# A hybrid encoder layer pair on one core: two more value blocks fed unsplit to TensorE, and the order of splits, gelu parts, scans and small stores moved

## The chip, the core and the metric

The kernel runs on one core of a Trainium2 chip. TensorE (PE) multiplies, VectorE (DVE) and ScalarE (ACT) do the elementwise work, GpSimd (POOL) sums squares for the norms, and SyncE (SP) issues nearly all transfers. Each engine runs its own instructions in the order in which they are written and waits at counting semaphores. The metric is the time of one execution on the device, in microseconds (us); lower is better.

## The reference, cut to what matters

Input x is 256 tokens by 2048 channels, float32. There are two layers. Each is a normed mixer and a normed MLP of hidden size 8192, with residual sums. The change touches the first mixer only:

```python
proj = xn @ w_in                                   # 2048 -> q, k, v, u of 1024 each
q, k, v, u = jnp.split(proj, [A_WIDTH, 2 * A_WIDTH, 3 * A_WIDTH], axis=-1)
o_a = dilated_attention(heads(q), heads(k), heads(v), t5_table)      # 8 heads, T5 bias
y = (s5_direction(ug, ..., False) + s5_direction(ug, ..., True) + d_skip * ug)
y = jax.nn.gelu(y)                                 # S5 state space, both directions
o_b = y * jax.nn.sigmoid(y @ w_glu)
return jnp.concatenate([o_a, o_b], axis=-1) @ w_out
```

## The kernel before, in words

All weights stream through one ring of four slots, `raw[:, s]`, 512 KB each. A **block** is 256 columns of a weight matrix and has four **parts**, s = 0 to 3, each with four slices of 128 of the contraction. Part number n is 4 * block + s. SP loads part n into slot n % 4 once the part before it in that slot is done with (`raw_slot`).

Most parts are **split** before use: ACT copies `raw` to a rounded high half in `whl` (`high`, L556), DVE subtracts to get the low half (`low`, L926), and PE makes three reduced products in `sub_mm` (L1567). Parts of **native** blocks, J_NAT0 to J_NAT1 - 1, skip this: PE multiplies `raw` itself by the whole input `xf` (L1544), and no engine splits. `xf` is made once by `whole_input` on DVE, four additions, and lies over slots 0 and 1 of `whl`. So a split into these slots after the native blocks must wait until the last native part is used.

The first mixer goes through these stages:

- Blocks 0 to 3 project u, 4 to 7 q, 8 to 11 k, 12 to 15 v, 16 and 17 are the GLU (gate) matrix. Blocks 18 on are the output projection and all that follows.
- Meanwhile DVE makes the S5 weights and then the scan: 63 steps of four small operations (`scan`), a few after each part from (6, 3) to (12, 3) (`SCAN_SLOTS`). Between blocks 8 and 9 PE makes the local kernels (L1679), ACT takes them (`take_kernel`) and DVE adds the diagonal (`kernel_diagonal`, 0 and 1, counted in `k_mid`).
- SP writes these kernel rows to DRAM (`store_k`, tile `kst` to `k_rows`, waits for `k_mid` 6) and reads them back in another layout (`load_m`, to `mloc`, waits until the store has landed). Both stand in SP's one queue between weight loads, at a fixed n.
- In block 13, after each part, PE makes one **round** of chunk outputs (`chunk_outputs`, L1723 to L1732). Round 0 waits for the whole scan, `mloc` and the diagonal. ACT and DVE add the two directions (`take_round`, `round_sum`), SP stores the result (`store_y`) and loads it as `u` (`load_y`).
- Then the **head loop**, steps g = 0 to 7, one head of attention each. PE does parts of blocks 14 to 17 (`HEAD_SUBS`: two v parts a step, later two GLU parts), then scores of head g + 1, transposes of head g, and output of head g - 1. ACT and DVE split q, k and v of a head (`head_high`, `head_low`), do the softmax, split the weight parts, and do the gelu of the eight `u` tiles (`gelu_inner`, `gelu_tanhs`, `gelu_end`, and its split into `act` by ACT L839 and `gelu_low`). ACT also issues the T5 bias loads (`load_bias_a`). GLU part 64 needs gelu tiles 0 to 3 split and part 65 needs 4 to 7.

The whole order is written out by hand; no scheduler moves anything.

Of the kernel before, what the change touches and what calls it, by code (L numbers as in the profile page):

```python
# [18 lines left out]
HA = 8  # L19
# [7 lines left out]
NT = 8  # L27
# [30 lines left out]
J_NAT0, J_NAT1 = 8, 14  # L58
# [41 lines left out]


# [10 lines left out]
def build(nc, ins, out):  # L112
# [7 lines left out]
    with ctx:  # L120
# [180 lines left out]
        def _(sp):  # L301
# [110 lines left out]
            for n in range(4 * J_GLU + 8):  # L412
# [111 lines left out]
        def _(a):  # L524
# [229 lines left out]
            for s in range(4):  # L754
                high(0, J_HEADS, 0, s)
# [29 lines left out]
            def head_high(h):  # L785

                if h >= 3:
                    a.wait_ge(pv_mm, h - 2)
# [8 lines left out]
            high(0, J_HEADS + 1, 0, 0)  # L797
# [17 lines left out]

            for g in range(9):
                subs = HEAD_SUBS[g]
                for k, n in enumerate(subs):
                    if k == 1:
                        continue  # L820
                    high(0, n // 4 + 1, 0, n % 4)
                    if n in (4 * J_HEADS + 3, 4 * J_HEADS + 7):
                        take_tiles(n // 4)
# [6 lines left out]
                if len(subs) > 1 and subs[1] + 4 < 4 * J_OUT0 + 3:  # L830
                    high(0, subs[1] // 4 + 1, 0, subs[1] % 4)
                if g + 1 < HA:
                    scale_probs(g + 1)
                if g < 3:
                    gelu_tanhs(2 * g + 2)
                if g == 3:
                    for t in range(NT):
                        a.wait_ge(gelu_out, t + 1)
                        nc.scalar.activation(act[:, NT + t, 0, :], u[:, t], ACT.Copy, scale=0.5).then_inc(y_hi, 1)  # L839
# [3 lines left out]
                if g + 2 < HA:  # L843
                    head_high(g + 2)
# [76 lines left out]
        def _(v):  # L921
# [306 lines left out]
            def after(j, s):  # L1228
# [36 lines left out]
            for r in range(3):  # L1265
                round_sum(r)
            for s in range(4):
                low(0, J_HEADS, 0, s)
            round_sum(3)
# [69 lines left out]
            low(0, J_HEADS + 1, 0, 0)  # L1339
# [4 lines left out]
            for g in range(9):  # L1344
                subs = HEAD_SUBS[g]
                m = 2 * (g - 4)
                if subs:
                    low(0, subs[0] // 4 + 1, 0, subs[0] % 4)
# [8 lines left out]
                if len(subs) > 1 and subs[1] + 4 < 4 * J_OUT0 + 3:  # L1357
# [617 lines left out]
```

## Time and profile before

| | before |
|---|---|
| median of 3 runs | 2295.6 us (2291.8 to 2296.89) |
| the profiled execution's own time | 2293.73 us |
| its span in the trace | 2291.9 us |
| PE busy | 2225.5 us (97%) |
| DVE busy | 1561.0 us (68%) |
| ACT busy | 1025.6 us (45%) |
| first product of block 18 | at 369.2 us |

The page gives each engine's busy time as a share of the span. From block 18 on PE is busy all the time until the last few microseconds; what the change can alter lies ahead of it, in the first 370 us. "PEclk" in a row is the clock that TensorE was granted, as a share of 2.4 GHz; it has two levels, 1.00 and 0.50, and a value between is a mix over the stretch.

### The profile page before, as it was taken

The numbers are of one execution on the slowest core, as the hardware profiler recorded it, in microseconds if no ns is written. First come the engines' busy times: TensorE is split into PE (matmuls) and PEld (weight loads), VectorE is DVE, ScalarE is ACT, GpSimd is POOL, SyncE is SP. The second block draws the span as 40 slices with busy tenths as digits, with TensorE's granted clock in tenths as the row PEclk, the third lists the DMA queues.
The fourth block names the chain that finished last, engine by engine and source line by source line (L and its number), as shares of the span: only waits on it lengthen the run. The fifth ranks groups of instructions, "written<-read, shape, count | busy, mean of one in ns | idle before, by whom it ended". The sixth has DMA issues, their size and how long they took to land.

```text
span 2291.9 us, 40651 instructions
## 1 busy us (share of the span) xinstructions
PE 2225.5 (97%) x14099; PEld 1965.7 (86%) x14099; DVE 1561.0 (68%) x2549; ACT 1025.6 (45%) x1473; POOL 166.7 (7%) x154
## 2 busy tenths in 40 slices
PE   6989879999999999999999999999999999999997
PEld 6988668888888888888888888888888888888886
DVE  7799267676567567567677777767756756756765
ACT  6620157544444444444455444454444444444442
POOL 1000001400000000000320000141000000000022
PEclk9999889999999999999999999999999999999999
DMA  8535654657557557656665656565666565666563
GB/s 225 167 105 152 126 177 146 189 188 211 187 189 205 189 188 203 196 188 199 195 199 164 202 169 196 166 192 184 192 192 192 184 192 184 192 192 192 184 191 112
DMA packets 438953, 418.02 MB, mean 182 GB/s; under 512 B 49627, under 2 KB 434859, under 8 KB 438348
## 3 DMA queue, kind: packets, MB, share of 16 engines
q1 hardware_dynamic: 435952, 414.30, 59.3%
q10 hardware_dynamic: 2908, 2.51, 0.4%
q8 instruction: 55, 0.90, 0.2%
q14 instruction: 38, 0.31, 0.0%
HBM read 406.35 MB, written 10.39 MB: 182 GB/s over the span
## 4 chain that ended last, share of the span: by engine, by line
PE 92%; DVE 4%; ACT 1%; DMA 1%; issue 1%; SPq 0%; ACTq 0%; DVEq 0%
PE psum L1570 54%; PE psum L1571 27%; PE psum L1544 4%; PE psum L1567 2%; PE psum L1746 1%; DVE whl L926 1%; DVE fa L926 1%; ACT whl L556 0%; PE psum L1728 0%; DMA xin<-in_x 0%; SPq L382 0%; PE psum L1766 0%; DMA raw<-in_ab_w_in 0%; DVE ysum L926 0%; PE psum L1723 0%
## 5 line engine op out<-in xcount | busy, mean ns | idle before, releaser
L926 DVE TENSOR_TENSOR whl<-raw,whl 128x1024 fp32r<-128x1024 f32 x720 | 887.8, 1244 | 495.5 <-ACT whl L556 493.6
L556 ACT ACTIVATE whl<-raw 128x1024 fp32r<-128x1024 f32 x720 | 763.5, 1061 | 759.0 <-PE psum L1571 683.4
L1570 PE MATMUL psum<-act,whl 128*128 128x512 f32 x2560 | 892.4, 394 | 0.0
L1571 PE MATMUL psum<-act,whl 128*128 128x256 f32 x2560 | 713.6, 279 | 0.0
L1570 PE MATMUL psum<-hid,whl 128*128 128x512 f32 x2048 | 710.3, 392 | 0.0
L1570 PEld LDWEIGHTS psum<-act,whl 128*128 128x128 f32 x2560 | 479.7, 187 | 109.4
L1571 PE MATMUL psum<-hid,whl 128*128 128x256 f32 x2048 | 570.4, 279 | 0.0
L1571 PEld LDWEIGHTS psum<-act,whl 128*128 128x128 f32 x2560 | 482.1, 188 | 0.1
L1570 PEld LDWEIGHTS psum<-hid,whl 128*128 128x128 f32 x2048 | 383.5, 187 | 86.8
L1571 PEld LDWEIGHTS psum<-hid,whl 128*128 128x128 f32 x2048 | 385.5, 188 | 0.0
L567 ACT ACTIVATE half<-psum 128x256 f32<-128x256 f32 x344 | 113.7, 382 | 286.0 <-PE psum L1571 285.1
L926 DVE TENSOR_TENSOR ysum<-psum,half 128x256 f32<-128x256 f32 x344 | 130.0, 419 | 159.1 <-ACT half L567 159.0
L1567 PE MATMUL psum<-act,whl 128*128 128x256 f32 x768 | 98.3, 287 | 0.0
L489 POOL TENSOR_TENSOR ssum<-x 128x256 f32<-128x256 f32 x4 | 2.9, 728 | 1295.1 <-DVE x L926 1295.1
L1567 PEld LDWEIGHTS psum<-act,whl 128*128 128x128 f32 x768 | 94.4, 193 | 0.8 <-ACT unat L716 0.8
L1570 PE MATMUL psum<-whl,act 128*128 128x512 f32 x256 | 91.1, 398 | 0.0
L1570 PE MATMUL psum<-o_c,whl 128*128 128x512 f32 x256 | 89.2, 392 | 0.3 <-DVE o_c L926 0.3
L492 POOL TENSOR_TENSOR sq<-x 128x256 f32<-128x256 f32 x60 | 61.7, 1029 | 184.3 <-DVE x L926 179.7
L494 POOL TENSOR_TENSOR ssum<-ssum,sq 128x256 f32<-128x256 f32 x60 | 71.7, 1195 | 4.7
L1571 PE MATMUL psum<-whl,act 128*128 128x256 f32 x256 | 71.9, 281 | 0.0
L1571 PE MATMUL psum<-o_c,whl 128*128 128x256 f32 x256 | 71.6, 280 | 0.0
L1544 PE MATMUL psum<-xf,raw 128*128 128x256 f32 x256 | 59.8, 392 | 7.6 <-DVE xf L926 7.6
(203 smaller groups left out, 1798.0 us busy)
## 6 DMA issues: line engine op xcount, KB each, us to landing
raw<-in_mlp_w SPq DMA_DIRECT2D x512, 512.0 KB, 4.0
raw<-in_c_w_qkv SPq DMA_DIRECT2D x96, 512.0 KB, 4.5
raw<-in_ab_w_in SPq DMA_DIRECT2D x64, 512.0 KB, 4.0
raw<-in_ab_w_out SPq DMA_DIRECT2D x32, 512.0 KB, 4.2
raw<-in_c_w_out SPq DMA_DIRECT2D x32, 512.0 KB, 4.4
raw<-in_s_w_glu SPq DMA_DIRECT2D x8, 512.0 KB, 3.4
bias_c<-rpb_pad SPq DMA_DIRECT2D x64, 64.0 KB, 2.5
rpb_pad<-rpbw SPq DMA_DIRECT2D x4, 889.0 KB, 10.7
```

Source lines behind the costliest of these rows:

```text
L489: nc.gpsimd.tensor_tensor(ssum[:], x[:, 0], x[:, 0], ALU.mult).then_inc(ssum_done, 1)
L492: nc.gpsimd.tensor_tensor(sq[:], x[:, kt], x[:, kt], ALU.mult).then_inc(sq_done, 1)
L494: nc.gpsimd.tensor_tensor(ssum[:], ssum[:], sq[:], ALU.add).then_inc(ssum_done, 1)
L556: nc.scalar.activation(whl[:, s, :, 0, :], raw[:, s], ACT.Copy).then_inc(hi_done, 1)
L567: nc.scalar.activation(half[:, n], psum[:, banks + n, T:2 * T], ACT.Copy).then_inc(half_done, 1)
L926: return nc.vector.tensor_tensor(dst, s0, s1, op)
L1544: last = pe.matmul(psum[:, banks + n, 0:T], w, m, start=(kt == 0), stop=(kt == KT - 1), skip_group_check=True)
L1567: last = pe.matmul(bank[:, 0:T], w, m, start=(first and c == 0), stop=(final and c == 2), skip_group_check=True)
L1570: pe.matmul(bank, *big, start=first, stop=False, skip_group_check=True)
L1571: last = pe.matmul(bank[:, 0:T], *little, start=False, stop=final, skip_group_check=True)
L1746: last = pe.matmul(dst, w(wp), m(mp), start=(c == 0 and p == 0), stop=(c == len(products) - 1 and p == 2), skip_group_check=True)
```

## The change

Blocks 14 and 15 become native (J_NAT1 is 16), so their eight parts are no longer split. On DVE `whole_input` goes from the third part of block 7 to the first, and the two diagonals go six and five parts forward. On SP `store_k` goes from part 52 to 45, `load_m` from 54 to 47, and the last `store_y` and `load_y` come a little sooner. In the head loop the split of head 2 comes ahead of the loop. The GLU parts that used slots of split v parts are now split in step 3, four at once. The gelu tiles are split two a step from step 1, with the last two in step 4.

```diff
-J_NAT0, J_NAT1 = 8, 14
+J_NAT0, J_NAT1 = 8, 16
+HEAD_SPLITS = [()] * 3 + [(4 * J_GLU, 4 * J_GLU + 1, 4 * J_GLU + 2, 4 * J_GLU + 3)]
+HEAD_SPLITS += [(4 * J_GLU + 2 * g + 4, 4 * J_GLU + 2 * g + 5) for g in range(3)] + [(4 * J_GLU + 10,), ()]
...
-                if n == 52:
+                if n == 45:
                     store_k()
-                if n == 54:
+                if n == 47:
                     load_m()
                 for r in range(NROUND):
-                    if n == (56, 57, 58, 60)[r]:
+                    if n == (56, 57, 58, 59)[r]:
                         store_y(r)
-                    if n == (58, 59, 61, 62)[r]:
+                    if n == (58, 59, 59, 59)[r]:
                         load_y(r)
...
-            high(0, J_HEADS + 1, 0, 0)
+            head_high(2)
...
             for g in range(9):
...
+                splits = HEAD_SPLITS[g]
+                early = len(splits) // 2 if len(splits) > 1 else len(splits)
+                if 2 <= g < HA - 1:
+                    head_high(g + 1)
+                if g in (1, 3):
+                    take_tiles(J_HEADS + g // 2)
+                for n in splits[:early]:
+                    high(0, n // 4, 0, n % 4)
...
+                if 1 <= g <= 3:
+                    y_high(2 * g - 2)
...
-                if (j, s) == (10, 2):
+                if (j, s) == (9, 0):
                     kernel_diagonal(0)
-                if (j, s) == (11, 2):
+                if (j, s) == (10, 1):
                     kernel_diagonal(1)
...
-                    if j + 1 == J_NAT0 and s == 2:
+                    if j + 1 == J_NAT0 and s == 0:
                         whole_input()
...
+                if 2 <= g < HA - 1:
+                    head_low(g + 1)
+                for n in splits[:early]:
+                    low(0, n // 4, 0, n % 4)
+                if g == 4:
+                    gelu_low(6)
+                    gelu_low(7)
                 if g + 1 < HA:
                     scores(g + 1, (g + 1) % 2, ss_a, bias_a, False)
```

SP's queue around the kernel rows, before. "raw<-in_ab_w_in" is a weight part, x4 four of them; "t_rel" is the T5 table, stored after parts 41 and 45.

```order
40 L405 DMA t_rel<-t5sb 128x512
41 L334 DMA raw<-in_ab_w_in 128x4x256 x4
42 L405 DMA t_rel<-t5sb 128x512
43 L334 DMA raw<-in_ab_w_in 128x4x256 x3
44 L364 DMA k_rows<-kst 16x16x112 x4
45 L334 DMA raw<-in_ab_w_in 128x4x256 x2
46 L373 DMA mloc<-k_rows 16x32x64 x8
47 L334 DMA raw<-in_ab_w_in 128x4x256 x2
```

The same place in the changed kernel; its first row is the T5 store after part 45.

```order
40 L409 DMA t_rel<-t5sb 128x512
41 L368 DMA k_rows<-kst 16x16x112 x4
42 L338 DMA raw<-in_ab_w_in 128x4x256 x2
43 L377 DMA mloc<-k_rows 16x32x64 x8
44 L338 DMA raw<-in_ab_w_in 128x4x256 x2
45 L409 DMA t_rel<-t5sb 128x512
46 L338 DMA raw<-in_ab_w_in 128x4x256 x7
```

The four stores now stand ahead of the loads of parts 46 and 47, and the eight reads ahead of those of parts 48 and 49. Before, the parts behind them were 52 and 53, and 54 and 55.

DVE from the end of head step 3 to the scores of head 5, before: `act<-u` is the low half of a gelu tile (L929), `whl` the low half of a weight part.

```order
416 L926 TENSOR_TENSOR o_s<-psum,o_s 128x256
417 L929 SCALAR_TENSOR_TENSOR u<-inner,u 128x256 x2
418 L929 SCALAR_TENSOR_TENSOR act<-u,act 128x256 x8
419 L926 TENSOR_TENSOR qk_s<-qk_a,qk_s 128x2x256
420 L926 TENSOR_TENSOR v_s<-v_a,v_s 128x256
421 L926 TENSOR_TENSOR whl<-raw,whl 128x4x256
422 L929 SCALAR_TENSOR_TENSOR ss_a<-psum,bias_a 128x512
```

The same stretch in the changed kernel.

```order
409 L934 TENSOR_TENSOR o_s<-psum,o_s 128x256
410 L934 TENSOR_TENSOR whl<-raw,whl 128x4x256 x2
411 L937 SCALAR_TENSOR_TENSOR u<-inner,u 128x256 x2
412 L937 SCALAR_TENSOR_TENSOR act<-u,act 128x256 x2
413 L934 TENSOR_TENSOR qk_s<-qk_a,qk_s 128x2x256
414 L934 TENSOR_TENSOR v_s<-v_a,v_s 128x256
415 L934 TENSOR_TENSOR whl<-raw,whl 128x4x256
416 L937 SCALAR_TENSOR_TENSOR act<-u,act 128x256 x2
417 L937 SCALAR_TENSOR_TENSOR ss_a<-psum,bias_a 128x512
```

The last two gelu tiles (row 416) now stand behind the split of part 68 (row 415), where before all eight stood ahead of it, and two more weight parts (row 410) stand ahead of the last gelu products.

ACT at the end of a GLU step, before: `half` takes half a GLU tile, `ysum` is its tanh, `qk_s` and `v_s` are the high halves of the next head.

```order
185 L567 ACTIVATE half<-psum 128x256 x2
186 L789 ACTIVATE qk_s<-qk_a 128x2x256
187 L790 ACTIVATE v_s<-v_a 128x256
188 L763 DMA bias_a<-t_rel 128x256 x2
189 L850 ACTIVATE ysum<-ysum 128x256 x2
190 L556 ACTIVATE whl<-raw 128x4x256
```

The same place in the changed kernel.

```order
169 L571 ACTIVATE half<-psum 128x256 x2
170 L765 DMA bias_a<-t_rel 128x256 x2
171 L858 ACTIVATE ysum<-ysum 128x256 x2
172 L792 ACTIVATE qk_s<-qk_a 128x2x256
173 L793 ACTIVATE v_s<-v_a 128x256
174 L560 ACTIVATE whl<-raw 128x4x256
```

The head's split now stands behind the tanh, which waits for DVE.

## Rows read from the trace of the kernel before

**Rows 1.** Waits of PE, 140 to 376 us: total, times, longest.
```profile
PE psum L1746 <- DVE v_s L926: 15.2, 6, 5.8
...
PE psum L1544 <- DVE xf L926: 7.6, 1, 7.6
...
PE psum L1723 <- issue: 7.3, 1, 7.3
```

**Rows 2.** Chain of work, 135 to 160 us: start, length, what.
```profile
142.28 0.88 DVE ysum L926 x3
...
151.83 1.06 DVE xf L926
```

**Rows 3.** PE in order of time, blocks 8 to 13.
```profile
153.03 5.84 PE L1544 MATMUL psum<-xf,raw 128*128 128x256 f32 x16 [7.56 <-DVE xf L926]
...
159.75 3.72 PE L1544 MATMUL psum<-xf,raw 128*128 128x256 f32 x16
...
191.95 27.89 PE L1544 MATMUL psum<-xf,raw 128*128 128x256 f32 x128
219.68 17.43 PE L1544 MATMUL psum<-raw,xf 128*128 128x256 f32 x80
244.36 0.48 PE L1723 MATMUL psum<-u,mloc 128*64 128x64 f32 x4 [7.25 <-issue]
```

**Rows 4.** DVE in order of time, diagonals and the scan's last operation.
```profile
201.95 0.28 DVE L926 TENSOR_TENSOR kst<-em,di 128x128 f32<-128x128 f32 x1
...
216.55 0.27 DVE L926 TENSOR_TENSOR kst<-em,di 128x128 f32<-128x128 f32 x1
...
235.11 0.38 DVE L926 TENSOR_TENSOR wv<-ysum 128x128 f32<-128x128 f32 x1
```

**Rows 5.** SP's queue in order of time.
```profile
223.79 3.23 SPq L364 DMA_DIRECT2D k_rows<-kst  x4
...
230.67 7.86 SPq L373 DMA_DIRECT2D mloc<-k_rows  x8
238.57 2.26 SPq L334 DMA_DIRECT2D raw<-in_ab_w_in  x2
```

**Rows 6.** Issues, 226.5 to 228 us: count, KB each, us to landing.
```profile
raw<-in_ab_w_in SPq DMA_DIRECT2D x1, 512.0 KB, 5.3
k_rows<-kst SPq DMA_DIRECT2D x1, 112.0 KB, 4.2
```

**Rows 7.** Issues, 238 to 239.3 us.
```profile
raw<-in_ab_w_in SPq DMA_DIRECT2D x1, 512.0 KB, 7.2
```

**Rows 8.** Clock by stretch: PE, PEld, DVE, ACT, POOL busy, PEclk, DMA share, GB/s.
```profile
246.00:250.00 4.00, 4.00 (x80) 3.07 (x79) 0.00 (x0) 0.00 (x0) 0.00 (x0) 0.50 0.03 9
...
257.00:258.00 1.00, 1.00 (x6) 0.75 (x4) 0.00 (x0) 0.00 (x0) 0.00 (x0) 1.00 0.41 68
```

**Rows 9.** PE in order of time, block 13's third part and the first v part.
```profile
263.41 3.72 PE L1544 MATMUL psum<-raw,xf 128*128 128x256 f32 x16
...
281.21 3.02 PE L1567 MATMUL psum<-whl,act 128*128 128x256 f32 x23
```

**Rows 10.** Busy time by head step, columns as in rows 8.
```profile
287.35:295.46 8.11, 8.11 (x71) 8.11 (x70) 4.20 (x10) 4.28 (x10) 0.00 (x0) 1.00 0.70 202
295.46:307.24 11.78, 6.01 (x42) 5.81 (x41) 7.72 (x15) 5.99 (x14) 0.00 (x0) 0.87 0.87 299
307.24:317.92 10.68, 9.23 (x63) 9.03 (x63) 8.08 (x16) 6.31 (x14) 0.00 (x0) 0.83 0.38 121
...
329.27:341.97 12.70, 10.21 (x50) 8.96 (x49) 8.35 (x18) 7.17 (x19) 0.00 (x0) 0.78 0.43 146
...
350.68:359.38 8.70, 7.79 (x50) 6.76 (x50) 7.20 (x15) 6.62 (x17) 0.00 (x0) 1.00 0.50 151
```

**Rows 11.** DVE, costliest groups, 281 to 369 us: count, busy, mean ns, idle before.
```profile
L926 DVE TENSOR_TENSOR whl<-raw,whl 128x1024 fp32r<-128x1024 f32 x17 | 20.8, 1224 | 10.3 <-ACT whl L556 10.3
```

**Rows 12.** ACT, the same view and stretch.
```profile
L556 ACT ACTIVATE whl<-raw 128x1024 fp32r<-128x1024 f32 x16 | 16.8, 1049 | 5.5 <-DMA raw<-in_ab_w_in 3.2 <-PE psum L1799 2.3
```

More of the change, by code:

```diff
@@ L753, in _ @@
             take_tiles(J_HEADS - 1)
-            for s in range(4):
-                high(0, J_HEADS, 0, s)
             take_round(3)
@@ L785, in head_high @@
             def head_high(h):
+                a.wait_ge(tiles_out, 2 * (J_V + h // 2 + 1))
                 if h >= 3:
@@ L814, in _, with y_high @@
             gelu_tanhs(0)
+            def y_high(t0):
+                for t in (t0, t0 + 1):
+                    a.wait_ge(gelu_out, t + 1)
+                    nc.scalar.activation(act[:, NT + t, 0, :], u[:, t], ACT.Copy, scale=0.5).then_inc(y_hi, 1)
             for g in range(9):
[L817 to L823, printed above, removed]
+                splits = HEAD_SPLITS[g]
[6 more added lines that the diff above has]
+                    high(0, n // 4, 0, n % 4)
                 if g < HA:
@@ L829, in _ @@
                     out_high(g - 1, (g - 1) % 2, o_s[:, g - 1, 0, :])
-                if len(subs) > 1 and subs[1] + 4 < 4 * J_OUT0 + 3:
-                    high(0, subs[1] // 4 + 1, 0, subs[1] % 4)
+                for n in splits[early:]:
+                    high(0, n // 4, 0, n % 4)
                 if g + 1 < HA:
                     scale_probs(g + 1)
+                if 1 <= g <= 3:
+                    y_high(2 * g - 2)
                 if g < 3:
@@ L836, in _ @@
                 if g == 3:
-                    for t in range(NT):
-                        a.wait_ge(gelu_out, t + 1)
-                        nc.scalar.activation(act[:, NT + t, 0, :], u[:, t], ACT.Copy, scale=0.5).then_inc(y_hi, 1)
+                    y_high(6)
                 m = 2 * (g - 4)
@@ L843, in _ @@
                 if g + 2 < HA:
-                    head_high(g + 2)
                     a.wait_ge(sc_sum, g + 1)
@@ L1264, in _ @@
                     after(j, s)
-            for r in range(3):
+            for r in range(NROUND):
                 round_sum(r)
-            for s in range(4):
-                low(0, J_HEADS, 0, s)
-            round_sum(3)
             def scores(hh, b, ss, bias, masked):
@@ L1338, in _ @@
             head_low(1)
-            low(0, J_HEADS + 1, 0, 0)
+            head_low(2)
             scores(0, 0, ss_a, bias_a, False)
@@ L1344, in _ @@
             for g in range(9):
-                subs = HEAD_SUBS[g]
+                splits = HEAD_SPLITS[g]
+                early = len(splits) // 2 if len(splits) > 1 else len(splits)
                 m = 2 * (g - 4)
-                if subs:
-                    low(0, subs[0] // 4 + 1, 0, subs[0] % 4)
+                if 2 <= g < HA - 1:
[5 more added lines that the diff above has]
+                    gelu_low(7)
                 if g + 1 < HA:
@@ L1356, in _ @@
                     out_low(g - 1, (g - 1) % 2, o_s[:, g - 1, 1, :], o_s[:, g - 1, 0, :])
-                if len(subs) > 1 and subs[1] + 4 < 4 * J_OUT0 + 3:
-                    low(0, subs[1] // 4 + 1, 0, subs[1] % 4)
+                for n in splits[early:]:
+                    low(0, n // 4, 0, n % 4)
                 if g < 4:
@@ L1364, in _ @@
                     gelu_inner(2 * g + 3)
-                if g == 3:
-                    for t in range(NT):
-                        gelu_low(t)
+                if 1 <= g <= 3:
+                    gelu_low(2 * g - 2)
+                    gelu_low(2 * g - 1)
                 if 4 <= g < 8:
@@ L1372, in _ @@
                         tile_sum(0, J_GLU + m // 4, 0, n, ysum[:, n], glu_group=m // 2 % 2)
-                if g + 2 < HA:
-                    head_low(g + 2)
                 if 4 <= g < 8:
```

## The prediction, made before the changed kernel ran

> **What bounds the kernel now.** I first asked for the time at which PE stops waiting for good. From the first product of block 18, at 369.2 us, nothing in the diff moves any instruction, so the change is worth what it moves that moment. Ahead of it the waits of PE, by what ended them, name three gaps [rows 1]: 7.6 us in one piece for `xf`, 7.3 us in one piece put down to "issue", and 15.2 us in six pieces for the splits of the heads.
>
> PE in order of time places them [rows 3]. Block 8 starts at 153.03 after 7.56 us of waiting. Blocks 8 to 13 then run without a gap until 237.11, and round 0 starts at 244.36. DVE had ended the scan at 235.5 [rows 4]. The eight reads of `mloc` were issued from 230.67 to 238.53 [rows 5], so it is they that were late. The head loop is the third place: from 281.21 to 369.18, 88.0 us, in which no engine is full [rows 10]. A step is a chain: scores, exponentials, gelu, the next head's split, the next scores.
>
> The clock counts too. After the 7.56 us wait the first part of block 8 takes 5.84 us, where the next takes 3.72 [rows 3], at 0.50 of the clock. After the 7.25 us wait the clock is still 0.50 at 250 us and back at 1.00 at 257 [rows 8].
>
> **xf earlier.** DVE begins the scan at 142.28 and now makes `xf` after two steps rather than seven [rows 2]. A step is (216.55 - 201.95 - 0.85) / 10 = 1.38 us, 0.85 being a diagonal's three operations of 0.28 [rows 4]. So `xf` starts at 145.0, 6.8 us before 151.83, and PE starts block 8 at 146.2. Its wait falls from 7.6 to about 0.8 us, too short for the clock to drop by any row here, which saves another 2.1 (5.84 - 3.72). PE is 8.9 us ahead through blocks 8, 9 and 10. DVE does the same work in another order, so the scan still ends at 235.5. That is a floor under round 0: with nothing else in the way PE would come to it at 228.2 and wait.
>
> **Kernel rows earlier.** Something else is in the way. A native part takes 27.89 / 8 = 3.49 us [rows 3]. Block 10 starts at 191.95 - 8.9 = 183.05, its second part is used at 190.0, and SP can load part 45. Then SP stands at `store_k` until the second diagonal. This now comes after step 37 instead of 50, with the other diagonal also ahead of it: 216.55 - 13 x 1.38 = 198.6, done at 199.5. So parts 46 and 47, whose slots come free at 193.5 and 197.0, wait behind it. The four stores take 3.23 us to issue [rows 5], part 46 is issued at 202.8 and lands 5.3 us later [rows 6], at 208.1. PE wants it after block 10 and two parts of block 11, at 183.05 + 6 x 3.49 = 204.0. **PE waits 4.1 us**, and is at the end of block 11 at 215.1.
>
> Next, `load_m` waits for the stores, 4.2 us after the last issue [rows 6], until about 206.4. Its eight reads take 7.86 us to issue [rows 5], so part 48 is issued at 214.3 though its slot was free at 200.5, and it lands 7.2 us later, as the part behind the same reads did before [rows 5, 7]: 221.5. **PE waits 6.4 us** from 215.1. A wait of that length let the clock fall twice; I take the smaller of the two prices, 2.1 us, since here too dense parts follow [rows 3]. Parts 49 to 52 land faster than PE uses them. PE ends the first part of block 13 at 221.5 + 5 x 3.49 + 2.1 = 241.1, and round 0 starts there: `mloc` and the scan are long in. Against 244.36 that is **3.3 us gained**. Without the waits it would be 235.6 (8.8 gained). With the clock down already in the first wait, and as long as after 237, it is about 245 (nothing gained).
>
> The order of transfers can be checked against the Trainium skill, "DMA: Bandwidth & Descriptors", section "Queues, rings and completion order": descriptors of one issuing engine are consumed in ring order. The trace agrees so far as the part behind the reads took 7.2 us, and the one behind the four stores 5.3. By that rule the only way for part 48 to be early would be for the reads themselves to be quick.
>
> **Rounds.** PE now comes to round 0 straight from matmuls, at full clock. From 263.41 to 281.21 lie two parts and two rounds, 17.8 us [rows 9]; with 3.65 for a part, a round is 5.25. From 244.36 to 263.41 lie two rounds and a part, which took 19.05 and should take 14.15. **4.9 us gained** (bounds 0, if the clock is down again, and 4.9). The later `store_y` and `load_y` serve gelu tiles 4 to 7, wanted some 20 us after they land, so they cost nothing. If that cover went, SP's last store (waiting for round 3) would hold the loads of parts 60 to 63 by some 8 us; PE needs part 60 only after seven products' worth of work, 16 us on.
>
> So the first v part begins at 281.21 - 3.3 - 4.9 = 273.0.
>
> **The head loop.** Removed: eight ACT copies of 1.05 us and eight DVE subtractions of 1.22 [rows 11, 12]. Added on PE: a native v part is 3.49 against 3.02 us [rows 3, 9], 0.46 x 8 = 3.7 us, hidden behind the waits of rows 1 in all but the first steps. A page of the Trainium skill speaks louder against it: "FP8 and Floating Point Precision", section "TensorE Precision Notes", gives true float32 four passes through the array, where a split part makes three reduced products. By that estimate a native part costs 4/3 of a split one, 8.1 us in all for the eight; the row shows 3.49 / 3.02 = 1.16, and I go by the row.
>
> Each number below is for a step from scores to scores. Opening, 281.21 to 287.35: 6.1 becomes about 4.8, since no split stands ahead of the heads. Steps 0 to 2 take 8.1, 11.8 and 10.7 [rows 10]. In each a split stands in the chain, one copy, one subtraction less the work that overlaps it, about 1.9 us; without it 7.5 (PE's two native parts bound it), 9.3 (the bias load bounds it) and 8.8. Together with the opening, 6.3 us gained. Step 3 gains about 0.8. Step 4 loses: between its scores and the next there now stand three splits instead of one (2 x 1.05), four gelu copies on ACT (1.6) and the low halves of the last two tiles behind part 68's split, and only then can PE begin part 65. I get 14.7 us by adding them up, against 12.7 [rows 10], with PE idle for about 9 in one piece, so the clock falls and the GLU part that follows takes 2.8 longer (PE's 7.8 us of a GLU step [rows 10] less some 2.2 for the head, halved): 17.5, a loss of 4.8. Steps 5 and 6 take 8.7 now [rows 10]; the head's high half stands behind the tanh, 0.8 us more each, and the end some 0.4: 2.0 lost. Sum: 6.3 + 0.8 - 4.8 - 2.0 = +0.3, call it **nothing**. Bounds: 4 gained if the clock stays up in step 4, 4 lost if it stays down through step 5. That "heads are made a step sooner" changes little in itself: from head 3 on the split stands at the start of a step where it stood at the end of the one before.
>
> **Sum.** 3.3 + 4.9 + 0 = 8.2 us. The profiled execution took 2293.73, 1.9 below the median of the runs, so 2285.5 for one like it and 2295.6 - 8.2 = **2287.4** for the median.
>
> **The rivals.**
>
> 1. *The loads do not hold PE.* If the reads of `mloc` move faster than before, or parts 48 and on do not queue behind them, round 0 goes by the scan, 235.6: 8.8 + 4.9 = 13.7 gained, up to 17 with the head loop: 2279 to 2282. For it: the reads met two weight loads in flight before. Against it: they meet the same two now, and rows 7.
>
> 2. *The waits only move.* Both waits in blocks 11 and 12 lower the clock, and step 4 costs all I fear and more. Gain 0 to 4.6, time 2291 to 2295.6. For it: the head waits of under 6 us already show a mean clock of 0.78 to 0.87 [rows 10].
>
> 3. *Slower.* Place: the four GLU steps. PE's work in such a step is 7.8 us at full clock [rows 10] and 15.6 at half, over the 9.5 of the chain. If step 4's long wait puts the clock down for three steps, PE becomes the bound: 3 x (15.6 - 9.5) = 18 lost, net 10 slower, 2305. It decides once the low level lasts over two steps, 12 us lost. Against it: the longest low stretch seen, after 237 us, was over by 257 [rows 8].
>
> **How the numbers follow.** The forecast (gain 5 to 12) 0.50, rival 1 0.20, rival 2 0.22, rival 3 0.08. A measurement of this kernel tells about 0.2%, 4.6 us, from no change. Faster: 0.50 + 0.20 + 0.04 of rival 2 = 0.74. Same: 0.18. Slower: 0.08. The range runs from rival 1's middle, 2279.5, to the middle of rival 2, 2293.5.
>
> **What would show it.** `xf` at 145, block 8 at 146, first part 3.7 us. PE waits of about 4 us at 204 and 6 us at 215 for weight loads. Round 0 near 241 at clock 1.00. First v part near 273, PE idle some 9 us before part 65, block 18 near 361. It is wrong if block 12 starts without a wait, if round 0 comes at 235.6 or after 244, or if the head loop is off 88 us by over 4.

## The result, and the profile after

The changed kernel takes 2278.88 us (median of 4 executions, 2276.11 to 2280.05). The kernel before, run beside it, takes 2293.7 us (4 executions, 2291.3 to 2296.89). The ratio is 0.9933 with a 95% interval of 0.9915 to 0.995: 14.8 us faster, where the forecast said 8.2. The profiled execution has a span of 2276.6 us against 2291.9. One execution of the version all_ahead below took 3691.34 us at a mean clock of 0.558; it has no trace and is left out of every figure.

The waits of PE between 140 and 376 us come first (in all, times, longest). They answer to [rows 1].

```profile
PE psum L1755 <- DVE v_s L934: 7.0, 3, 4.0
PE psum L1553 <- DMA raw<-in_ab_w_in: 6.7, 2, 3.8
PE psum L1806 <- DVE act L937: 4.9, 2, 3.8
PE psum L1755 <- DVE pt_a L934: 1.1, 1, 1.1
PE psum L1553 <- ACT qk_a L720: 0.7, 1, 0.7
```

The waits for `xf` and the one put down to "issue" are gone. The waits for the splits of the heads fell from 15.2 to 7.0 us. Two kinds are new: 6.7 us for weight loads, and 4.9 us for `act`, the gelu tiles. PE in order of time says where they lie, and answers to [rows 3]:

```profile
145.51 3.69 PE L1553 MATMUL psum<-xf,raw 128*128 128x256 f32 x16 [0.71 <-ACT qk_a L720]
...
207.12 8.86 PE L1553 MATMUL psum<-xf,raw 128*128 128x256 f32 x32 [3.84 <-DMA raw<-in_ab_w_in]
218.85 17.50 PE L1553 MATMUL psum<-raw,xf 128*128 128x256 f32 x80 [2.88 <-DMA raw<-in_ab_w_in]
236.29 0.34 PE L1732 MATMUL psum<-u,mloc 128*64 128x64 f32 x4
...
268.23 3.72 PE L1553 MATMUL psum<-raw,xf 128*128 128x256 f32 x16
```

Block 8 starts at 145.51, 7.5 us earlier. PE waits twice, ahead of the last two parts of block 11 and ahead of block 12. Round 0 starts at 236.29, 8.07 us earlier, and the first v part at 268.23, 12.98 us earlier. The head loop ends where block 18 starts, at 352.17 against 369.18: 17.0 us, of which 4.0 are the loop's own (83.94 against 87.97 us).

SP's queue in order of time (start, length of the issue, count) answers to [rows 5], and two rows of DVE, a diagonal and the scan's last operation, to [rows 4]:

```profile
198.86 2.70 SPq L368 DMA_DIRECT2D k_rows<-kst  x4
201.61 1.89 SPq L338 DMA_DIRECT2D raw<-in_ab_w_in  x2
204.37 7.89 SPq L377 DMA_DIRECT2D mloc<-k_rows  x8
212.31 1.68 SPq L338 DMA_DIRECT2D raw<-in_ab_w_in  x2
```

```profile
197.88 0.27 DVE L934 TENSOR_TENSOR kst<-em,di 128x128 f32<-128x128 f32 x1
...
234.43 0.38 DVE L934 TENSOR_TENSOR wv<-ysum 128x128 f32<-128x128 f32 x1
```

SP stands still from 190.4 until the second diagonal is done, then issues the stores, part 46, the reads of `mloc`, and part 48 at 212.31, which PE uses at 218.85. The scan is through at 234.8, only 1.5 us ahead of round 0.

The last view is that of the clock, in the form of [rows 8] (stretch, PE, PEld, DVE, ACT, POOL busy, PEclk, DMA share, GB/s):

```profile
207.00:209.00 2.00, 1.88 (x5) 1.57 (x6) 1.93 (x7) 0.00 (x0) 0.00 (x0) 0.61 1.23 215
209.00:211.00 2.00, 2.00 (x6) 1.53 (x6) 1.90 (x7) 0.00 (x0) 0.00 (x0) 0.54 1.38 140
211.00:213.00 2.00, 2.00 (x11) 1.75 (x10) 1.90 (x7) 0.00 (x0) 0.00 (x0) 1.00 1.20 155
...
219.00:222.00 3.00, 3.00 (x15) 2.64 (x16) 2.83 (x10) 0.00 (x0) 0.00 (x0) 1.00 1.01 351
...
244.00:248.00 4.00, 4.00 (x90) 3.04 (x88) 0.00 (x0) 0.00 (x0) 0.00 (x0) 1.00 0.42 69
```

Behind the wait of 3.84 us the clock is near 0.5 (1.2 of 2.4 GHz) until about 211 us. Behind the wait of 2.88 us it is 1.00, and so it is in the rounds.

### The profile page after: what moved, and what is told of

Its sections match the earlier page's. It is cut to its first block, busy times and chain, and to the rows that moved or that the text cites. A ratio compares the mean times of both kernels' runs of the same rounds, so it can differ in the third digit from the quotient of the medians.

```text
span 2276.6 us, 40505 instructions
## 1 busy us (share of the span) xinstructions
PE 2225.2 (98%) x14035; PEld 1961.4 (86%) x14035; DVE 1551.7 (68%) x2541; ACT 1018.9 (45%) x1465; POOL 166.2 (7%) x154
## 4 chain that ended last, share of the span: by engine, by line
PE 91%; DVE 6%; DMA 1%; ACT 1%; issue 0%; SPq 0%; DVEq 0%; ACTq 0%
PE psum L1579 54%; PE psum L1580 28%; PE psum L1576 2%; PE psum L1553 2%; DVE ysum L934 2%; PE psum L1755 1%; DVE whl L934 1%; DVE fa L934 1%; DVE wv L934 1%; DMA raw<-in_ab_w_in 1%; PE psum L1737 0%; DMA bias_a<-t_rel 0%; PE psum L1806 0%; PE psum L1732 0%; PE psum L1775 0%
## 5 line engine op out<-in xcount | busy, mean ns | idle before, releaser
L934 DVE TENSOR_TENSOR whl<-raw,whl 128x1024 fp32r<-128x1024 f32 x712 | 878.0, 1244 | 486.2 <-ACT whl L560 484.4
L560 ACT ACTIVATE whl<-raw 128x1024 fp32r<-128x1024 f32 x712 | 754.9, 1061 | 754.4 <-PE psum L1580 682.6
```

Source lines behind the costliest of these rows:

```text
L560: nc.scalar.activation(whl[:, s, :, 0, :], raw[:, s], ACT.Copy).then_inc(hi_done, 1)
L934: return nc.vector.tensor_tensor(dst, s0, s1, op)
```

## The experiments: from `xf` to the rounds

Four kernels came first, to find how the gain divides. Each time below is read from the same rows as above; a ratio is against the kernel before, run beside it. Each kernel has one trace, so it matters how far traces differ by chance. Seven kernels of this study (the changed one and the six under "The experiments: the head loop") have the same code up to the head loop. Their round 0 starts between 233.98 and 237.35 us, and their first v part between 265.92 and 269.29. A difference of 3.4 us or less in where round 0 or the first v part starts shows nothing by itself. The time from round 0 to the first v part, by contrast, is 31.94 us in all seven.

**front_only.** The kernel before with the early `xf`, diagonals, stores and reads, and nothing else.

```diff
-                if n == 52:
+                if n == 45:
                     store_k()
-                if n == 54:
+                if n == 47:
                     load_m()
...
-                if (j, s) == (10, 2):
+                if (j, s) == (9, 0):
                     kernel_diagonal(0)
-                if (j, s) == (11, 2):
+                if (j, s) == (10, 1):
                     kernel_diagonal(1)
...
-                    if j + 1 == J_NAT0 and s == 2:
+                    if j + 1 == J_NAT0 and s == 0:
                         whole_input()
```

> The kernel before with only xf, diagonals, kernel rows and their reads moved forward; blocks 14 and 15 stay split and the head loop stays as it was. If the parts of the change add up, round 0 starts at 236.3 us and the first v part at 268.2 as in the changed kernel, the head loop keeps its 88.0 us, and block 18 starts at 356.2: 13.0 us gained. Rival: the unsplit v parts also matter ahead of the loop (their splits stood on ACT and DVE before the loop), then block 18 comes later than 357.

Measured: 2283.03 us, ratio 0.9946 (0.993 to 0.9963), 10.8 us faster. Its PE waits 3.53 and 2.15 us for the loads, starts round 0 at 235.33 and the first v part at 267.27, so up to there it has all of the gain, and the 1 us more is within chance. Block 18 starts at 357.47 instead of the expected 356.2, late enough for the rival's sign, but nothing shows that it is for the rival's reason: the rival put the loss ahead of the loop, and it is in it. The head loop is 90.2 us, 2.2 longer than before although nothing in it differs, 0.9 of it in step 0 and 1.2 in step 4. One piece can be seen: in step 4 the same wait for gelu (2.50 against 2.49 us) is followed by nine pairs of products at half clock, where the kernel before has five.

**loop_only.** The changed kernel with those numbers put back.

```diff
-                if n == 45:
+                if n == 52:
                     store_k()
-                if n == 47:
+                if n == 54:
                     load_m()
...
-                if (j, s) == (9, 0):
+                if (j, s) == (10, 2):
                     kernel_diagonal(0)
-                if (j, s) == (10, 1):
+                if (j, s) == (11, 2):
                     kernel_diagonal(1)
...
-                    if j + 1 == J_NAT0 and s == 0:
+                    if j + 1 == J_NAT0 and s == 2:
                         whole_input()
```

> The changed kernel with xf, diagonals, kernel rows and their reads back in their old places; blocks 14 and 15 unsplit and the new head loop. If the parts add up, the first v part starts at 281.2 as before, the loop takes 83.9 us as in the changed kernel, block 18 starts at 365.2: 4.0 us gained. Rival: the loop was shorter because the clock and the transfers found it in another state; then it takes 86 or more.

Measured: 2290.31 us, ratio 0.998 (0.997 to 0.9989), 3.5 us faster. Its head loop, from 277.58 to 362.28, is 84.7 us, near the changed kernel's 83.94, so the rival (86 or more) is out. In this trace the native v parts and the new order of the loop are worth 3.3 us by themselves. One thing was not expected: the first v part comes 3.6 us earlier than before, although the code ahead of it is that of the kernel before. SP took 6.73 us to issue the reads of `mloc` instead of 7.86, they took 5.7 us to land (median) instead of 7.0, and PE's wait ahead of round 0 is 5.15 us in place of 7.25. No edit accounts for it, so I take it for scatter between executions and credit it to neither part of the change.

**xf_late.** The changed kernel with `xf` made as late as before.

```diff
-                    if j + 1 == J_NAT0 and s == 0:
+                    if j + 1 == J_NAT0 and s == 2:
                         whole_input()
```

> The changed kernel with xf made at the third part of block 7 again. My reading: PE comes 8.6 us later to blocks 10 to 12, so both waits for weight loads (3.8 and 2.9 us) vanish and round 0 starts at 237.1 instead of 236.3: 0.8 us lost against the changed kernel, so early xf and early rows do not add. Rival: each is worth its own stall, then round 0 comes 7 to 9 us later, at 243 or after.

Measured: 2278.85 us, ratio 0.9928 (0.9912 to 0.9945). PE in order of time:

```profile
152.47 5.62 PE L1553 MATMUL psum<-xf,raw 128*128 128x256 f32 x16 [7.56 <-DVE xf L934]
...
220.54 17.50 PE L1553 MATMUL psum<-raw,xf 128*128 128x256 f32 x80 [1.47 <-DMA raw<-in_ab_w_in]
237.98 0.34 PE L1732 MATMUL psum<-u,mloc 128*64 128x64 f32 x4
```

The wait of 7.56 us for `xf`, and the first part at half clock behind it, are back, 9 us in all. Of the load waits one has vanished and the other is 1.47 us. Round 0 is 1.7 us later than in the changed kernel, 0.6 outside the range of the seven, and the median is the same. With early rows the early `xf` is worth 0 to 2 us, since SP's loads, and behind them the scan, hold PE a little later anyway. The rival (7 to 9 us later) is out.

**rows_late.** The changed kernel with the stores and reads put back, the diagonals left early.

```diff
-                if n == 45:
+                if n == 52:
                     store_k()
-                if n == 47:
+                if n == 54:
                     load_m()
```

> The changed kernel with the stores of the kernel rows back at part 52 and the reads at part 54; xf and diagonals stay early. My reading: PE is early and so part 54 comes early, the reads are issued at about 221 and land at 235, just after the scan (234.8). Round 0 starts at 235.5 but after a wait of about 6 us, so at clock 0.50: the rounds take 4.9 us more and the first v part starts at 272.3 instead of 268.2, 4 us lost against the changed kernel. Rival: the move of the rows is what removes the 7.3 us wait, then round 0 comes at 243 or later and 10 or more are lost.

These are again the places behind the loads of parts 52 and 54. So before, the stores stood ahead of parts 53 and 54 and the reads ahead of 55 and 56, one part further back than the section on the change says.

Measured: 2281.42 us, ratio 0.9939 (0.9922 to 0.9955). The median is 2.5 us above the changed kernel's, but the two intervals overlap; the trace is clearer. PE:

```profile
234.85 0.48 PE L1732 MATMUL psum<-u,mloc 128*64 128x64 f32 x4 [7.50 <-DVE wv L934]
...
243.23 6.05 PE L1553 MATMUL psum<-raw,xf 128*128 128x256 f32 x16
...
272.26 1.99 PE L1553 MATMUL psum<-raw,xf 128*128 128x256 f32 x8
```

Round 0 starts 1.4 us earlier than in the changed kernel, for it waits for nothing but the scan: with PE early, SP's queue is early too, and the reads are issued from 220.91 us instead of 230.67 although they stand where they stood. But PE has stood 7.50 us, the first four products of the round take 0.48 us in place of 0.34, the part behind it 6.05 in place of 3.72, and the first v part is 4.0 us later, as expected. What the early rows buy on top of the early `xf` is that PE comes to the rounds straight from matmuls.

**rows_loose.** To see whether the load waits are a loss: the stores two parts later, behind part 47's load, and the reads three parts later, behind part 50's.

```diff
-                if n == 45:
-                    store_k()
                 if n == 47:
+                    store_k()
+                if n == 50:
                     load_m()
```

> The changed kernel with the stores of the kernel rows two parts later (after part 46's load instead of ahead of it) and the reads of the block matrix three parts later. In the changed kernel SP stands at these stores and the loads of parts 46 and 48 come 3.8 and 2.9 us late for PE, but PE then comes to round 0 at 236.3 straight from matmuls at full clock. Theory (the two load waits cost little, because PE would otherwise wait for the scan, which ends at 234.4 to 235.1): PE's load waits are 0 to 1, it is at round 0 near 230 and waits 5 us there for the scan, round 0 starts near 235 at half clock, the first v part comes 1 to 4 us later than the changed kernel's 268.2; median 2280 to 2283. Rival (the load waits are a real loss): round 0 at 235 at full clock or soon back there, first v part at 267, 1.3 us gained, median near 2277.5.

Measured: 2280.78 us, ratio 0.9938 (0.9922 to 0.9955). PE waits 1.25 us for a load and then 5.87 for the scan:

```profile
221.12 7.17 PE L1553 MATMUL psum<-raw,xf 128*128 128x256 f32 x32 [1.25 <-DMA raw<-in_ab_w_in]
...
234.17 0.48 PE L1732 MATMUL psum<-u,mloc 128*64 128x64 f32 x4 [5.87 <-DVE wv L934]
...
242.54 4.47 PE L1553 MATMUL psum<-raw,xf 128*128 128x256 f32 x16
```

The first v part comes at 269.98, 1.75 us later than with the load waits and 0.7 later than in any of the seven. From round 0 to there it takes 35.8 us and not 31.94, which is beyond chance. The theory held and the rival (267, a gain) did not: no cost of the two load waits can be seen, they lie in place of a longer one that also costs clock.

**rows_blocked.** The suspected cost made larger: SP kept at the stores longer.

```diff
-                if (j, s) == (10, 1):
+                if (j, s) == (11, 0):
                     kernel_diagonal(1)
```

> The changed kernel with the second kernel diagonal made three slots of the scan later, so that SP stands at the stores of the kernel rows some 10.5 us longer: the suspected cost of the early rows, made larger. Theory (the loads of parts 46 and on stand behind SP's wait, and PE pays for it one for one): the stores are issued near 209.4 instead of 198.9, PE's wait for part 46 grows from 3.8 to 14 us, its wait for part 48 shrinks below 1 us, the clock is at half behind the long wait (a part of 5.8 us in place of 3.7), round 0 starts near 247 instead of 236.3 and the first v part near 279; about 10.5 us lost, median near 2289.5. Rival (part 46 is late by its own landing time and not by SP's wait): round 0 stays within 2 us of 236.3 and the median near 2280.

Measured: 2288.16 us, ratio 0.9979 (0.997 to 0.9988). SP's queue, then PE:

```profile
209.59 2.66 SPq L368 DMA_DIRECT2D k_rows<-kst  x4
212.29 1.89 SPq L338 DMA_DIRECT2D raw<-in_ab_w_in  x2
```

```profile
217.96 10.11 PE L1553 MATMUL psum<-xf,raw 128*128 128x256 f32 x32 [14.98 <-DMA raw<-in_ab_w_in]
229.15 17.51 PE L1553 MATMUL psum<-raw,xf 128*128 128x256 f32 x80 [1.07 <-DMA raw<-in_ab_w_in]
246.59 0.34 PE L1732 MATMUL psum<-u,mloc 128*64 128x64 f32 x4
```

The theory held in each place. The stores come 10.7 us later, PE's wait grows from 3.84 to 14.98, round 0 is 10.3 and block 18 10.0 us later (362.19). PE pays for SP's place in line one for one as soon as its load is the last thing to come. The first two parts behind the wait take 10.11 us where two parts at full clock take 6.98, and yet the sum hardly shows it: the wait for part 48 shrank to 1.07.

## The experiments: the head loop

Times of DVE's operation on the scores give the steps. In the changed kernel steps 0 to 6 are 7.04, 8.56, 9.55, 11.21, 14.52, 9.09 and 9.10 us, with 5.05 ahead of them and 9.82 behind; before they were 8.11, 11.78, 10.68, 11.35, 12.70, 8.71 and 8.70, with 6.14 and 9.80 [rows 10]. The changed kernel's loop stands unaltered in loop_only, xf_late, rows_late, rows_loose and rows_blocked too. Over these six traces every step but one agrees within 0.21 us. Step 4 is 14.36 to 14.52 in three and 15.19 to 15.57 in three, and the loop is 83.67 to 85.10 us. The longer form, as xf_late shows it, has its slow products behind the second wait for `act`, with no wait after them:

```profile
318.71 0.47 PE L1806 MATMUL psum<-act,whl 128*128 128x512 f32 x1 [3.52 <-DVE act L937]
...
322.75 0.80 PE L1806 MATMUL psum<-act,whl 128*128 128x512 f32 x1 [2.37 <-DVE act L937]
...
323.55 0.63 PE L1806 MATMUL psum<-act,whl 128*128 128x512 f32 x1
```

At full clock such a product takes 0.40 us.

**gelu_lump.** The gelu tiles' halves made in one piece at the end of step 3, as before.

```diff
-                if 1 <= g <= 3:
-                    y_high(2 * g - 2)
...
                 if g == 3:
-                    y_high(6)
+                    for t0 in range(0, NT, 2):
+                        y_high(t0)
...
-                if g == 4:
-                    gelu_low(6)
-                    gelu_low(7)
...
-                if 1 <= g <= 3:
-                    gelu_low(2 * g - 2)
-                    gelu_low(2 * g - 1)
+                if g == 3:
+                    for t in range(NT):
+                        gelu_low(t)
```

> The changed kernel with one part undone: the high and low halves of all eight gelu tiles are made in one piece at the end of step 3, as before the change, and not two tiles a step. In the changed kernel part 64 runs at 310.2 and part 65 at 316.9 to 322.5, and the scores of head 5 follow; ACT's scaling of the probabilities in step 3 ends at 315.0. Theory (the two-a-step order lets part 64 run early and keeps four tiles' work out of the longest step): with eight copies of 0.38 from 315.0 part 64 begins only near 317 and the scores of head 5 come near 324.5 instead of 322.5; 2 us slower than the changed kernel, median near 2281, and PE has one idle piece of 9 us or more. Rival (the chain of step 4 is head 5's split, which does not depend on where the copies stand, since the same eight copies are made by 316.9 or 318.1): 0 to 0.5 us slower, 2279. If the one idle piece lowers the clock over both GLU parts: 2.8 more, 2284.

Measured: 2279.69 us, ratio 0.9926 (0.991 to 0.9943). The median is within the noise of the changed kernel's. PE waits in one piece, and the clock falls:

```profile
317.40 0.77 PE L1802 MATMUL psum<-act,whl 128*128 128x512 f32 x1 [6.19 <-DVE act L936]
...
325.83 0.88 PE L1751 MATMUL psum<-qk_s 128*128 128x256 f32 x6
```

Step 4 is 16.63 us, 2.1 longer than in the changed kernel and 1.1 to 2.3 longer than in the six traces with its loop. The head loop, from 268.74 to 354.74, is 86.0. Two tiles a step are worth 1 to 2 us in the trace. The idle piece is 6.19 us where I had expected 9 or more.

**heads_old.** The splits of the heads where they stood before the change.

```diff
             head_high(1)
-            head_high(2)
...
-                if 2 <= g < HA - 1:
-                    head_high(g + 1)
...
                 if g + 2 < HA:
+                    head_high(g + 2)
                     a.wait_ge(sc_sum, g + 1)
```

The low halves, `head_low`, are moved back in the same way.

> The changed kernel with one part undone: the split of a head stands where it stood before the change (head g+2 at the end of step g, in steps 4 and 5 ahead of the tanh), and not at the start of the next step. The prediction said that this part changes little in itself, except in steps 5 and 6, where the head's high half now stands behind the tanh. Theory: steps 0 to 4 stay within 0.5 us each, steps 5 and 6 become 0.6 to 0.9 shorter each, so block 18 starts 1.2 to 1.8 us earlier than the changed kernel's 352.17 and the median is near 2277.3. Rival (the step-sooner order is what made steps 0 to 2 short): steps 0 to 2 become 0.5 to 1 us longer each and the whole is 0 to 2 us slower, 2279 to 2281.

Measured: 2277.37 us, ratio 0.992 (0.9904 to 0.9937). The median is 1.5 us below the changed kernel's, which is within the noise; the steps are read more sharply. They are 7.53, 8.65, 9.30, 10.59, 14.45, 8.70 and 8.69, with 4.55 ahead, and the loop is 82.27 us. Steps 5 and 6 are 0.4 shorter each, half of what the prediction gave, and step 3 is 0.6 shorter, which it had not named. In the trace, heads a step sooner are a small loss, not a gain.

**gelu_ahead.** A new order against the two waits of step 4. In the changed kernel PE and DVE read there:

```profile
316.94 0.76 PE L1806 MATMUL psum<-act,whl 128*128 128x512 f32 x1 [3.77 <-DVE act L937]
317.50 0.41 PE L1808 MATMUL psum<-act,whl 128*128 128x256 f32 x1
...
320.96 0.50 PE L1806 MATMUL psum<-act,whl 128*128 128x512 f32 x1 [1.12 <-DVE act L937]
```

```profile
313.42 2.36 DVE L934 TENSOR_TENSOR whl<-raw,whl 128x1024 fp32r<-128x1024 f32 x2 [0.53 <-ACT whl L560]
315.70 0.75 DVE L937 SCALAR_TENSOR_TENSOR u<-inner,u 128x256 f32<-128x256 f32 x2
316.37 0.75 DVE L937 SCALAR_TENSOR_TENSOR act<-u,act 128x256 fp32r<-128x256 f32 x2
...
320.49 0.75 DVE L937 SCALAR_TENSOR_TENSOR act<-u,act 128x256 fp32r<-128x256 f32 x2
```

PE has finished part 64 at 313.1 and waits for `act` of tiles 4 and 5, which DVE makes only behind the split of parts 66 and 67, 2.36 us long, that nobody wants before the next step. Tiles 6 and 7 stand behind one split more. The new order makes the halves of tiles 4 to 7 first:

```diff
                 for n in splits[:early]:
                     high(0, n // 4, 0, n % 4)
+                if g == 3:
+                    y_high(6)
...
-                if 1 <= g <= 3:
+                if 1 <= g <= 2:
                     y_high(2 * g - 2)
...
                     gelu_tanhs(2 * g + 2)
-                if g == 3:
-                    y_high(6)
+                if g == 2:
+                    y_high(4)
...
+                if g == 3:
+                    gelu_end(6)
+                    gelu_end(7)
                 if 2 <= g < HA - 1:
                     head_low(g + 1)
...
-                if g == 4:
-                    gelu_low(6)
-                    gelu_low(7)
...
+                if g == 3:
+                    for t in range(4, NT):
+                        gelu_low(t)
                 for n in splits[early:]:
                     low(0, n // 4, 0, n % 4)
-                if g < 4:
+                if g < 3:
                     gelu_end(2 * g)
                     gelu_end(2 * g + 1)
...
-                if 1 <= g <= 3:
+                if 1 <= g <= 2:
                     gelu_low(2 * g - 2)
                     gelu_low(2 * g - 1)
```

> A new order on top of the changed kernel, against the two idle pieces of PE (3.8 and 1.1 us) that stand in step 4 ahead of the two halves of part 65. The copies and low halves of gelu tiles 4 to 7 are made in step 3, ahead of the splits of parts 66 and 67, and not behind them. Theory (part 65 waits only for the gelu tiles): part 65 follows part 64 within 1.5 us, the scores of head 5 come near 318.5 instead of 322.5, step 3 is 0 to 1 us longer, block 18 starts 3 to 4 us earlier, median near 2275.5. Rival 1 (head 5's split, made at 319.4, is nearly as late): the scores come no earlier than 320.5, 2 us gained, 2277. Rival 2 (the copies hold the splits that follow, and part 66 waits for them in the next step): nothing gained, 2279.

Measured: 2272.79 us, ratio 0.9902 (0.9886 to 0.9919), 6.1 us faster than the changed kernel; its slowest execution (2273.34) is faster than the changed kernel's fastest (2276.11). DVE's operation on the scores of heads 4 and 5, and PE's scores of head 5:

```profile
307.91 0.68 DVE L939 SCALAR_TENSOR_TENSOR ss_a<-psum,bias_a 128x512 f32<-128x512 f32 x1
...
316.78 0.69 DVE L939 SCALAR_TENSOR_TENSOR ss_a<-psum,bias_a 128x512 f32<-128x512 f32 x1
```

```profile
315.76 0.98 PE L1760 MATMUL psum<-qk_s 128*128 128x256 f32 x6 [1.07 <-DVE v_s L936]
```

Step 4 is 8.87 us in place of 14.52, and no wait for `act` is left. The head loop, from 266.53 to 344.77, is 78.24 us, 5.7 shorter. The direction was expected and the size was not: I had counted with 3 to 4 us. Two things were left out of that count: the clock hardly falls in this step (a mean of 0.96 against 0.88), and head 5's split itself comes earlier: ACT begins it at 313.30, 46.8 us behind the first v part, where in the changed kernel it is 49.2 (317.43). How the 5.7 us divide between the two was not measured.

**both_ahead, all_ahead, old_ahead.** Three versions on top of it: the heads' splits of steps 4 and 5 ahead of the gate's tanh; the same with the bias issued earlier; and instead of these the heads' splits all as before the change.

```diff
-                if 2 <= g < HA - 1:
+                if 2 <= g < 5:
                     head_high(g + 1)
...
                 if g + 2 < HA:
+                    if g >= 4:
+                        head_high(g + 2)
                     a.wait_ge(sc_sum, g + 1)
```

DVE's `head_low` is moved to match. For all_ahead, the first of these edits, `head_low` as there, and this:

```diff
                     scale_probs(g + 1)
+                if g + 2 < HA:
+                    a.wait_ge(sc_sum, g + 1)
+                    load_bias_a(g + 2)
...
-                if g + 2 < HA:
-                    a.wait_ge(sc_sum, g + 1)
-                    load_bias_a(g + 2)
+                if 4 <= g < HA - 2:
+                    head_high(g + 2)
```

For old_ahead the edit is that of heads_old.

> gelu_ahead with one thing more: in steps 4 and 5 the split of the head stands ahead of the tanh of the gate, as before the change, and no longer behind the first split of the next step. By heads_old against the changed kernel each of steps 5 and 6 is 0.4 us shorter so (8.70 and 8.69 against 9.09 and 9.10). Theory: 0.8 us off gelu_ahead's head loop (78.2 us from the first v part to block 18), median near 2272. Rival (PE is the bound in these steps, since its own work in one is 7.8 us): nothing gained.

> both_ahead with the two transfers of the bias of head g+2 issued right behind the scaling of the probabilities, ahead of gelu's tanh. In the changed kernel the bias for the third head is issued at 285.35, behind a tanh that waited for DVE, and DVE waits 3.58 us for scores and bias at 288.88, 0.8 us after the scores themselves are there. Theory: step 1 is 0.7 us shorter, the other steps unchanged, median near 2271.3. Rival (issuing two transfers holds ACT for 0.5 to 0.9 us and the tanh behind them is later by that): gelu tiles later by 0.5 us a step, nothing gained or 1 us lost.

> gelu_ahead with the heads' splits all where they stood before the change (head g+2 at the end of step g). heads_old against the changed kernel: steps 4.55, 7.53, 8.65, 9.30, 10.59, 14.45, 8.70, 8.69 against 5.05, 7.04, 8.56, 9.55, 11.21, 14.52, 9.09, 9.10, in all 1.7 us shorter. Theory (the two edits add up): head loop 1.7 us shorter than gelu_ahead's 78.2, median near 2271.1. Rival (gelu_ahead already used the idle time that the old order frees): no better than both_ahead, 2272.

Measured, in this order: 2271.71 us, ratio 0.9903 (0.989 to 0.9917); 2270.77, ratio 0.9902 (0.9887 to 0.9917); 2270.59, ratio 0.9904 (0.9889 to 0.9919). The head loops are 77.6, 76.4 and 77.2 us against 78.2: 0.6, 1.9 and 1.0 shorter, where 0.8, 1.5 and 1.7 were expected. The signs are as expected, but with these runs no version can be told from gelu_ahead by its time. All four beat both kernels, the changed one by 6 to 8 us.

## Why the prediction was right or wrong, point by point

- **What bounds the kernel, and that block 18 is the end of it.** Right. Block 18 starts 17.0 us earlier and the span is 15.3 shorter. Over the kernels of this study the stretch behind that moment varies between 1922 and 1926 us, so the difference of 1.7 is within what single executions scatter.
- **xf earlier.** Right in each number: `xf` at 144.15 (145.0), block 8 at 145.51 (146.2), the first part 3.69 us (3.7).
- **Kernel rows earlier.** The mechanism is right: both loads hold PE, and rows_blocked shows that they do it through SP's place in line. The wait for part 46 is 3.84 us, forecast 4.1. Rival 1 is out as a mechanism and came nearer as a number: it had the first v part 13.7 us earlier (measured 13.0) and a time of 2279 to 2282, for the waits turned out so short that PE reached round 0 only 1.5 us behind the scan. The Trainium skill, "DMA: Bandwidth & Descriptors", section "Queues, rings and completion order", states that each transfer engine consumes the descriptors of one issuer in ring order, and also that a later transfer may still finish first. Here it did not: the last read, issued at 211.6, took 5.9 us to land, and part 48, issued at 212.31, took 6.4.
- **The step that failed: "PE waits 6.4 us" for part 48, and the clock behind it.** The wait is 2.88 us. Part 48 was used at 218.85, not at 221.5: its issue was at 212.31 instead of 214.3, mainly because I had taken the stores' 3.23 us of issue and 4.2 of landing from the kernel before. There the reads start 6.9 us behind the first store, here 5.5. The transfers moved 202 GB/s around the stores there and 90 here, a likely reason that no run tested. From its issue to its use part 48 took 6.5 us for 7.2. The 2.1 us that I put on PE's clock behind this wait are not there: 80 products take 17.50 us, and 17.43 with no wait at all [rows 3]. Together 2.65 + 2.1 = 4.8 us: round 0 at 236.29 for 241.1, the whole error of this term, and more than the 3.4 us of chance.
- **Where the clock loss really was.** Behind the first, 3.84 us wait: two parts took 8.86 instead of 6.98. I had said that the clock would fall behind the wait of 6.4 and had given none to that of 4.1. It cost nothing, because part 48 was what PE had to wait for next. The loss went into that wait, as the 3.1 us did in rows_blocked.
- **Rounds.** Right: from round 0 to the first v part 31.94 us against 36.85, 4.9 gained as forecast. rows_late and rows_loose show why: 37.4 and 35.8 us where PE came from a wait of 7.50 or 5.87.
- **The head loop, "nothing".** Wrong by 4.0 us, and by 2.9 to 4.3 over the six traces with this loop. The largest part is step 4, "a loss of 4.8": forecast 17.5, measured 14.52, a loss of 1.8. The 14.7 us of the chain came near, though the prediction does not show its addition; what failed is "PE idle for about 9 in one piece, so the clock falls and the GLU part that follows takes 2.8 longer". Tiles 4 and 5 were ready long before 6 and 7, so PE stood 3.77 and 1.12 us, with four pairs of products between them, and the slow clock of those pairs was hidden by the wait that followed. Where the four pairs behind the second wait are the slow ones, no wait follows and the step is longer: 15.19 to 15.57 us in loop_only, xf_late and rows_loose, against 14.36 to 14.52 in the other three with this loop. gelu_lump, where the wait is one of 6.19, shows what I had feared in part: 16.63 us. Steps 5 and 6 lose 0.4 each and not 0.8. The other steps differ from the forecast by +0.25, -0.5, -0.7, +0.75, +0.7 and at the end -0.4, and nearly cancel.
- **Native v parts.** PE's busy time in the loop grew from 68.5 to 70.9 us, by 2.4 where 3.7 was forecast for the products alone; the mean clock rose from 0.90 to 0.94 at the same time, so the two do not compare directly. The loop became shorter all the same, so the work was hidden.
- **Whether the parts add.** front_only and loop_only gain 11.7 and 6.9 us at block 18, together 18.6, the change 17.0. Since 3.6 of the 6.9 lie ahead of the loop, where loop_only has nothing changed, these traces cannot tell. Early `xf` and early rows certainly do not add: both lead to the same floor, the scan's end, and with either one alone (xf_late, rows_late) the first v part comes 1.7 and 4.0 us later than with both.
- **Rival 2 and rival 3.** Both out: only the first of the two load waits lowered the clock, the rounds ran at full clock, and step 4 lost 1.8 us. Behind step 4 no GLU step stayed slow, steps 5 and 6 are 9.1 us.

## What to carry to other kernels

A drop of the clock is worth its price only if nothing is waited for behind it: before adding it to a sum, look at which wait comes next, and put it into that wait first. Two edits that remove waits ahead of the same floor are priced together, each against what the other leaves. In a step that is a chain, look at what the waited-for engine does just before: here the split of parts wanted a step later stood ahead of the tiles wanted now, and changing places gave 6 us, 0.3%, for no work less.

## What the runs showed that I had not expected

- Waits of PE between dense matmuls and what followed. After 1.47, 2.15, 2.88 and 3.27 us (xf_late, front_only, changed, gelu_lump) the next 80 products took 17.50 us each time, full clock. After 3.53, 3.84, 4.79 and 14.98 us (front_only, changed, heads_old, rows_blocked) the next 32 took 8.86, 8.86, 9.67 and 10.11 us where 6.98 is full clock. The prediction had looked only at the waits of 7.25 and 7.56 us [rows 3].
- The same wait does not cost the same each time: in step 4, 2.5 us of waiting, after work that was already slow, left nine slow pairs of products in front_only and five before. Behind 2.37 us, in xf_late, there are four. So the list above speaks of waits between dense matmuls alone.
